# A two-block transformer kernel: the eight bias rows are spread to 128 DRAM rows from a DRAM tensor instead of from SBUF partitions

## The reference

```python
s = jnp.einsum('bqhd,bkd->bqhk', qi, k_idx).astype(jnp.float32) * (IDX_DIM ** -0.5)
score = jnp.einsum('bqhk,bqh->bqk', jax.nn.relu(s), wi.astype(jnp.float32) * (IDX_HEADS ** -0.5))
...
_, idx = lax.top_k(score, topk)
...
logits = jnp.einsum('bqhd,bqkhd->bhqk', qb, k_sel).astype(jnp.float32) * scale
bias = rel_bias[t5_bucket(idx - qpos[None, :, None])]
logits = logits + jnp.transpose(bias, (0, 3, 1, 2)).astype(jnp.float32)
```

## Time and profile before

| what | before |
|---|---|
| median of 3 runs | 1158.39 us (1157.86 to 1159.93) |
| the profiled execution, device time | 1159.55 us |
| its span, from the first to the last instruction | 1157.8 us |
| mean granted TensorE clock | 0.963 of full speed |
| TensorE matmuls busy | 1058.3 us, 91% |
| VectorE busy | 624.7 us, 54% |
| ScalarE (ACT) busy | 473.9 us, 41% |
| GpSimd busy | 261.5 us, 23% |
| DMA queue of SP, share of 16 engines | 33.1% |

### The profile page before, as it was taken

How to read it: one execution, slowest core, us unless ns; L and a number is a source line. 1 busy time by engine, 2 the same in 40 slices (tenths; PEclk the granted TensorE clock), 3 DMA queues, 4 the chain that set the end, 5 groups by cost and what they waited for, 6 DMA issues and landing times.

```text
span 1157.8 us, 13434 instructions
## 1 busy us (share of the span) xinstructions
PE 1058.3 (91%) x5124; PEld 848.2 (73%) x5132; DVE 624.7 (54%) x1038; ACT 473.9 (41%) x819; POOL 261.5 (23%) x158
## 2 busy tenths in 40 slices
PE   7799999999999999999999985169999999999995
PEld 5596787677888888888887764157787766788884
DVE  5756566656444433454444563258755665425544
ACT  6634355454322311232344662025674545423332
POOL 0672332131110000101133330012332322331101
PEclk9899999999999999999999996679999999999998
DMA  7031232213223332322323289861132233222321
GB/s 279 20 110 37 69 97 74 74 55 108 93 92 104 103 102 73 110 91 91 109 91 121 59 91 49 46 104 56 57 117 73 83 109 91 73 91 91 106 94 73
DMA packets 33903, 103.35 MB, mean 89 GB/s; under 512 B 4568, under 2 KB 5992, under 8 KB 33840
## 3 DMA queue, kind: packets, MB, share of 16 engines
q1 hardware_dynamic: 33840, 102.49, 33.1%
HBM read 91.78 MB, written 4.72 MB: 83 GB/s over the span
## 4 chain that ended last, share of the span: by engine, by line
PE 70%; DVE 12%; ACT 5%; DMA 5%; SPq 5%; issue 3%; POOL 0%; DVEq 0%; ACTq 0%; POOLq 0%
PE bank L1341 19%; PE bank L1343 19%; PE bank L1342 19%; DMA WS<-wall 5%; SPq L1305 2%; PE bank L1473 2%; PE bank L1464 2%; PE bank L1353 2%; PE bank L1355 1%; PE bank L1354 1%; DVE score L2016 1%; DVE m L2014 1%; ACT WH L1511 1%; DVE f_s L1804 1%; PE bank L1445 1%
## 5 line engine op out<-in xcount | busy, mean ns | idle before, releaser
L1341 PE MATMUL bank<-HH,WH 128*128 128x512 f32 x808 | 331.6, 410 | 16.3 <-DVE WL L1760 8.5
L1343 PE MATMUL bank<-HH,WL 128*128 128x512 f32 x808 | 319.2, 395 | 0.0
L1342 PE MATMUL bank<-HL,WH 128*128 128x512 f32 x808 | 318.9, 395 | 0.0
L2085 POOL TENSOR_TENSOR WL<-WS,WH 128x1024 fp32r<-128x1024 f32 x64 | 154.7, 2417 | 407.1 <-ACT WH L1511 406.7
L1511 ACT ACTIVATE WH<-WS 128x1024 fp32r<-128x1024 f32 x164 | 170.7, 1048 | 115.6 <-DMA WS<-wall 73.9
L1341 PEld LDWEIGHTS bank<-HH,WH 128*128 128x128 f32 x808 | 155.0, 192 | 53.9 <-DVE WL L1760 8.5
L1343 PEld LDWEIGHTS bank<-HH,WL 128*128 128x128 f32 x808 | 153.9, 190 | 33.5
L1342 PEld LDWEIGHTS bank<-HL,WH 128*128 128x128 f32 x808 | 154.6, 191 | 29.4 <-issue 1.0
L1760 DVE TENSOR_TENSOR WL<-WS,WH 128x1024 fp32r<-128x1024 f32 x100 | 132.8, 1334 | 30.7 <-ACT WH L1511 30.6
L2138 POOL TENSOR_TENSOR fa<-fa,fg 128x512 f32<-128x512 f32 x22 | 28.3, 1285 | 273.4 <-DVE fa L1951 273.4
L1342 PE MATMUL bank<-GL,WH 128*128 128x512 f32 x176 | 68.5, 389 | 0.0
(11 more groups left out here) (336 smaller groups left out, 1755.3 us busy)
## 6 DMA issues: line engine op xcount, KB each, us to landing
WS<-wall SPq DMA_DIRECT2D x164, 512.0 KB, 3.4
scratch<-brow SPq DMA_DIRECT2D x8, 320.0 KB, 27.1
X<-xT SPq DMA_DIRECT2D x8, 256.0 KB, 6.9
b_t<-scratch SPq DMA_DIRECT2D x8, 256.0 KB, 3.7
b_m<-b_m SPq DMA_DIRECT2D x11, 128.0 KB, 4.2
outT<-X SPq DMA_DIRECT2D x5, 256.0 KB, 2.3
f_s<-f_s SPq DMA_DIRECT2D x8, 128.0 KB
f_m<-f_m SPq DMA_DIRECT2D x8, 128.0 KB
```

The lines of the kernel that those rows point to most:

```text
L1341: e.matmul(b[:, :], wh, xh[:, at_k, :], start=k == 0, stop=False)
L1342: e.matmul(b[:, :], wh, xl[:, at_k, :], start=False, stop=False)
L1343: m = e.matmul(b[:, :], wl, xh[:, at_k, :], start=False, stop=k == n - 1)
L2085: e.tensor_tensor(WL[:, u % NW, :], WS[:, u % NST, :], f32(WH[:, u % NW, :]), ALU.subtract).then_inc(*tick(w_low_g, u))
```

## The change

The eight rows of `brow` are first written to a new DRAM tensor `rows` of shape (8, 640), by one DMA (20 KB) of a new step `row_out`. The eight copies to `scratch` then read their row from `rows`, 128 times each, and wait for that DMA (`row_out`) instead of for ACT (`row_a`). They write the same bytes to the same places. ACT's write of `YAH` now waits for `row_out` in place of the eight copies.

```diff
+        rows = nc.dram_tensor("rows", (8, REL), F32, kind="Internal").ap()
...
-        rope_in = signal("rope_in", 16)
+        rope_in, row_out = signal("rope_in", 16), signal("row_out", 16)
...
             bias_rows()
+            do("row_out")
             for c in range(3):
...
+                elif kind == "row_out":
+                    q.wait_ge(row_a(1))
+                    e.dma_start(rows, brow[:, :]).then_inc(*row_out.tick())
                 elif kind == "copy_rows":
                     for hd in s["heads"]:
-                        src = brow[hd:hd + 1, :]
-                        src = bass.AP(tensor=src.tensor, offset=src.offset, ap=[src.ap[0], [0, 128], [1, REL]])
-                        q.wait_ge(row_a(1))
+                        src = rows[hd:hd + 1, :]
+                        src = bass.AP(tensor=src.tensor, offset=src.offset, ap=[[0, 128], [1, REL]])
+                        q.wait_ge(row_out())
                         e.dma_start(scratch[hd, :, :], src).then_inc(*copies_out[hd].tick())
...
-            q.wait_ge(y_out(), *(copies_out[hd]() for hd in range(8)))
+            q.wait_ge(y_out(), row_out(), *(copies_out[hd]() for hd in range(8)))
...
-                        q.wait_ge(gated_v(s["u"]), *(copies_out[hd]() for hd in range(8)))
+                        q.wait_ge(gated_v(s["u"]), row_out())
                         e.activation(YAH[:, p, :], t1[:, :], ACT.Copy).then_inc(*hi.tick(("ya", p)))
```

## The result

| | before | after |
|---|---|---|
| median, runs of this comparison | 1159.16 us (1157.86 to 1160.57) | 1110.12 us (1108.93 to 1112.66) |
| profiled execution: span, mean clock | 1157.8 us, 0.963 | 1108.8 us, 0.984 |
| SP's DMA queue, share of 16 engines | 33.1% | 28.3% |

The ratio is 0.958, with a 95% interval of 0.9558 to 0.9601: 49 us less, against a forecast of 1110 us (1103 to 1132).

A forecast was written before the change was run, and what follows sets the result against it. The prediction took TensorE to bound the kernel, except where one-partition copies in the DMA queue hold it; 46.9 + 6.6 - 4.7 = 48.8 us off 1158.4 gave 1110 us, range 1103 to 1132.

The forecast's parts named there:

- What bounds the stage: From 672 to 768 us, eight copies reading one SBUF partition, 11.8 us each, fill the DMA queue and delay weight loads.
- The three waits: TensorE's idle times of 13.61, 24.51 and 8.74 us behind late weight loads go if copies are quick: 46.9 us.
- VectorE is late next: Before its `uq` product TensorE waits 3.2 us for VectorE's second `a_q`; with 1.5 us of clock, minus 4.7 us.
- The clock: TensorE's lowered clock after the three idle times is given back: 6.6 us; the new pause takes 1.5 us.
- `rows<-brow`: The added 20 KB DMA lands 2.3 to 5.7 us after the loads issued at 670.11, about 676 us; cost nothing.
- The copies: Eight copies from DRAM take 1.9 us each, twice the lower bound of 0.94, and are hidden up to 4.2 us.
- How slow a copy may be: Copies stay hidden up to 4.2 us (78 GB/s); beyond, each us a copy costs between 6.4 and 8 us.
- A: Rival: VectorE becomes the bound of this stage, 6 to 14 us of the gain go, about 1120 us; chance 0.14.
- B: Rival: the DRAM row is slow in part, 7.3 us a copy, about 1130 us; chance 0.11.
- C: Rival: the short DRAM row is served slower than the partition, 14.2 us a copy, about 1178 us; chance 0.10.
- D: Rival: the 2560-byte writes to `scratch` are slow, not the source, so nothing changes, 1158 us; chance 0.03.
- The sum: Waits 46.9 plus clock 6.6 minus VectorE's 4.7 is 48.8 us less, from 1158.4 to 1109.6 us.

The follow-up runs named there:

- the copies out of `X`: Changed kernel, but the eight copies read 128 partitions of the SBUF tile X in place of one DRAM row: 1110.57 us, ratio 0.9594.
- The repeated comparison: The changed kernel once more, unedited, beside the kernel before on the same chip: 1112.54 us, ratio 0.9606.

## Why the prediction was right

**What bounds the stage: right.** The copies' source was the slow side, and its 11.8 us a copy is the rate of a path that four neighbouring partitions share. I had argued it from one partition alone; partitions 0 to 3 read together moved no more, 26 GB/s.

**The three waits, 46.9 us: right.** They are 0.37 us, 1.19 + 3.07 = 4.26 us and 0 now.

**VectorE is late next: right, and a little too small.** 3.2 us were summed, 1.19 + 3.07 = 4.26 measured. The sum took VectorE's work from the stalled kernel, where one of the two additions ran undisturbed (753.78 less 746.03 is 7.75 us). With the load on time, GpSimd's subtraction falls on the second addition as well: from 704.88 to 713.89 it is now 9.0 us.

**The clock: right.** The sum gave back 6.6 us and took 1.5 for the new pause, 5.1 in all; TensorE's matmuls between the marks are busy 4.7 us less. From 713.95 to 722.00 us, behind the wait of 3.07, TensorE was granted 0.79, 1.7 us lost where 1.5 were put down, and 1.00 from 722 to 812.6 us. In the kernel before it was 0.91 over the 30.4 us after the last stall.

**`rows<-brow`: right.** It landed 4.0 us after its issue, against the 2.3 to 5.7 us of the bounds, and delayed no load that anything waited for.

**The copies: hidden, as summed, but their size was off.** 1.9 us was twice the lower bound. The changed kernel's DMA share gives 1.06 us as a mean, many in a row 1.3, and only a first group 1.9. It did not matter, as all are below what fits.

**How slow a copy may be: the limit of 4.2 us was some tenths too high.** The sum had ACT want the second load at 708.7 us and the third at 720 on the old time line. On the new one, which is 2.6 us earlier, ACT took them at 702.78 and 707.66, so some 3 and 10 us earlier than that. By the same formula, with 672.53 as the start, that is an estimate of 3.9 us for the second load and 3.1 for the third, or 3.6 with the 3.7 us that the third could be late at no cost. The runs bracket the limit and no more: at 3.2 us a copy (102 GB/s) nothing was lost between the marks; at four times 1.3 to 1.9, so 5.2 to 7.6 us for each head, it was 10.0 us, where the prediction's 6.4 us for each us above 4.2 gives 6 to 22. For the first load, 23.6 us of slow copies made it 3.1 us late and 35.4 us made it 14.2 us late.

**The rivals.** A, VectorE, came to 1 us of what it was given 6 to 14 for. B and C, a slow DRAM row, did not come: a copy takes the queue 1.3 us in a long run, which is 250 GB/s, and 1.9 us or 172 GB/s in a first group, with the same 2560 bytes read 128 times. The Trainium skill ("SBUF — State Buffer", section "A bandwidth-pool intuition that's wrong (but worth ruling out)") puts a port of HBM at about 22.5 GB/s. The copies were not held to that; over how many ports a row is spread, no run here shows. D, the writes, fell with the copies out of `X`.

**The sum.** 48.8 us forecast, 46.5 us measured between the two marks of the stage. The 2.3 us are 1.9 of idle time (43.7 less was forecast, 41.8 measured) and 0.4 of clock (5.1 and 4.7). Three waits make up the idle part: the two for `a_q` are 1.1 us longer than summed, 0.37 us of the first stall stayed, and one of 0.88 us for ACT's `Pc` at 734.69 is new; a wait of 0.80 us for VectorE's `zb` became 0.40. The difference of the medians, 49.0 us, looks closer to the forecast than it is: in the profiled executions 2.6 us of it lie ahead of the stage, which is variation and luck. The repeated comparison gave 46.3.

## What to carry to other kernels

A DMA that read one SBUF partition 128 times moved 27.9 GB/s here with sixteen engines, and four neighbouring partitions with four engines 26, and it takes the queue with it: all that is issued behind it, weights above all, is late by the sum. Put such a row into DRAM first, or spread the source: partitions 0, 4, 8 and 12 moved 102 GB/s, and other spacings were not run. What it costs is not its bytes but how late it makes the first load that is wanted: count the slack of each load behind it before and after, and expect the next engine in line, here VectorE, to take a part of what you gain. When a stall goes, work that was apart comes together; look for pairs of engines whose instructions stretch each other.

## What the runs showed of the hardware that was not expected

- Four engines that read partitions 0 to 3 moved 26 GB/s, and the same four on partitions 0, 4, 8 and 12 moved 102, so 25.5 GB/s for each engine, more than the sixteenth of 349 GB/s (22) that I had estimated.
- Reads of the same 2560 bytes of DRAM, 128 times a copy, ran at 250 GB/s in a long run of copies and at 172 in a first group of twelve. Why the first group is slower, no run shows.
- A VectorE addition of two SBUF tiles (128x256) takes 0.47 us alone and 1.8 to 2.4 us while GpSimd subtracts a weight unit. Moving five of GpSimd's subtractions to VectorE lowered VectorE's own busy time, by 4.1 us.
- Two slow copies in front of an uncritical load made the stage 3.4 us shorter in the profile, by moving that collision: a wait of 3.07 us became 1.12, and with it went a stretch at a granted clock of 0.79.
